# A mixture-of-experts layer in split precision: 14 expert blocks with 64 token rows, high and low parts side by side

## The chip, the cores and the metric

The kernel runs on one NeuronCore of a Trainium2 chip. Time is device microseconds from start to end of one execution; lower is better. One execution is recorded by the hardware profiler, instruction by instruction: PE is the matrix engine (TensorE), PEld its weight loads, DVE the vector engine, ACT the scalar engine, POOL the GpSimd engine, SP the engine that issues most DMAs.

## What is computed

One layer of a decoder on 512 tokens of 1024 features, all in float32: three kinds of attention, an output projection with residual, and then a mixture of experts with top 4 of 32 experts, residual and a final RMSNorm. The change touches the mixture alone:

```python
logits = (xf @ w_router + b_router)
top_v, top_e = lax.top_k(logits, 4); gates = jax.nn.softmax(top_v, axis=-1)
# for every expert e, over the tokens that chose it:
gu = xe @ w_gu[e] + b_gu[e]                  # 1024 -> 2048
gate = jnp.minimum(gu[..., 0::2], 7.0)
up = jnp.clip(gu[..., 1::2], -7.0, 7.0)
act = (up + 1.0) * (gate * jax.nn.sigmoid(gate * 1.702))
y = act @ w_dn[e] + b_dn[e]                  # 1024 -> 1024, times the gate, added to the token
```

The 2048 pairs of token and expert are spread unevenly: 38 to 177 tokens to an expert, 64 on average.

## The kernel before

**Precision.** A float32 product is made of three products in the format fp32r. Both factors are split: the high part is the value rounded to fp32r by a copy, the low part is what is left. `three` (lines 1319 to 1323) adds high x high, high x low and low x high into one PSUM bank of 512 columns. The token rows are the stationary factor, 128 rows wide; the weights stream through.

**Blocks.** An expert's tokens are cut into blocks of at most 128. Which block belongs to which expert is worked out on the core: DVE counts tokens (line 1122 on), numbers the blocks, and the tables `exp_i`, `tok_i`, `gate_t` and `y_row_i` tell for each block its expert, its tokens, their gates and where the rows of the result go. There are at least 32 blocks; `loops` is the number of the last one.

**Halves.** A block's weights come as 12 pieces of 128 x 2048, called halves: 8 of gate/up (one k tile of 128 rows each) and 4 of down (two k tiles each). Each goes the same way. SP loads it into one of six slots of `raw` (1 MB); ACT rounds it into one of four slots of `w_hi` (`hi_m`, line 605); DVE writes raw minus high into `w_lo` (`lo_m`, line 873); PE runs 12 matmuls with it (`gate_up` line 1576, `down` line 1619). `lo_ready` frees the raw slot and releases PE; `half_used` frees the w_hi and w_lo slot.

**One iteration b** of the loop over blocks runs, on every engine in an order written out by hand, the gate/up of block b and the down of block b - 1:

- PE (`one_block`, line 1644): 8 halves of gate/up into the four banks of `gu_psum`, after the third the eight transposes of `act` (`turn_acts`); the bias (`gu_bias`, then `gu_done`); the eight transposes of the next block's token rows (`turn_rows`); 4 halves of down into two banks of `turn_psum`. Before the next iteration it waits on `sig_ready`, for gate/up overwrites the banks that the sigmoid reads.
- ACT (lines 804 to 816): `hi_m` 4 to 6, the high part of the turned act (`turn_act`, two pieces), `hi_m` 7 to 11, the sigmoid, the high part of the turned tokens (`turn_x`), `hi_m` 12 to 15 (the first four of the next iteration), and `y_out`, which scales the down result by the gate into `y_row`.
- DVE (lines 1255 to 1268): `lo_m` 4 to 6, the low part of the turned act, `lo_m` 7 to 10, `clamp` (two passes over gate/up), `lo_m` 11, the low part of the turned tokens, `activate`, `lo_m` 12 to 15.
- POOL (lines 582 to 586): gathers the token rows of block b + 1, loads the biases of block b, and scatters `y_row` of block b - 1 to `expert_rows` when `y_free` says it is ready.

The last block and the sum of the four rows of each token follow the loop.

## Time and profile before

| | |
|---|---|
| runs | 1488.14 us median of 3 (1487.26 to 1488.17) |
| the profiled execution, first to last instruction | 1485.0 us, 21394 instructions |
| PE busy | 1443.0 us (97%), 7006 matmuls |
| DVE busy | 1304.8 us (88%) |
| ACT busy | 1017.6 us (69%) |
| POOL busy | 274.3 us (18%) |
| moved by DMA | 472.64 MB |

Busy time is the union of an engine's instructions; a matmul's own duration is longer than the distance to the next one, since they are pipelined. "Idle before, releaser" names what ended the wait. Granted clock 1.00 is TensorE's 2.4 GHz, 0.50 is 1.2 GHz. A DMA share is the busy share of the core's 16 DMA engines in a stretch; a packet counts where it ends, so it can pass 1.

### The profile page before, as it was taken

The page shows a single profiled execution, that of the slowest core. Times are in us where ns is not written, and L with a number is a line of the kernel's source. Part 1 is how long each engine was busy: PE and PEld are TensorE (multiplying, and loading weights), DVE is VectorE, ACT ScalarE, POOL GpSimd, SP SyncE. Part 2 cuts the span into 40 slices and gives each one's busy share as a digit, 9 for nine tenths or more (in the row PEclk, how much of TensorE's full clock was granted, in tenths as well). Part 3 has the DMA queues.
Part 4 walks back from the last instruction along what each step waited for, and adds up shares of the span by engine and source line. Part 5 has one row for each costly group of instructions (what it writes and reads, how often), then busy time and mean ns, then how long its engine had stood idle before and what let it go on. Part 6 is the DMA issues. An engine that isn't in the chain of part 4 may idle for free.

```text
span 1485.0 us, 21394 instructions
## 1 busy us (share of the span) xinstructions
PE 1443.0 (97%) x7006; PEld 1173.1 (79%) x7006; DVE 1304.8 (88%) x1230; ACT 1017.6 (69%) x913; POOL 274.3 (18%) x282
## 2 busy tenths in 40 slices
PE   6999999899999999999999999999999999999996
PEld 6877866878888888888888888888888888888883
DVE  7358575899999999999999999999999999999998
ACT  6344345377777777777777777777777777777772
POOL 0000000033222222222222232222222222222210
PEclk9999999899999999999999999999999999999998
DMA  9411130499999999999999999999999999999994
GB/s 349 143 58 57 34 142 15 180 327 391 377 388 375 373 379 374 376 367 372 367 370 375 375 377 365 377 377 378 376 377 377 375 375 375 370 377 362 373 378 178
DMA packets 102334, 472.64 MB, mean 318 GB/s; under 512 B 16499, under 2 KB 16539, under 8 KB 68000
## 3 DMA queue, kind: packets, MB, share of 16 engines
q1 hardware_dynamic: 87632, 451.71, 78.0%
q0 software_dynamic: 14672, 20.53, 3.9%
q8 instruction: 18, 0.29, 0.1%
q14 instruction: 12, 0.10, 0.0%
HBM read 467.70 MB, written 22.02 MB: 330 GB/s over the span
## 4 chain that ended last, share of the span: by engine, by line
PE 92%; DVE 6%; DMA 1%; ACT 1%; issue 1%; SPq 0%; DVEq 0%
PE gu_bank L1321 18%; PE gu_bank L1322 18%; PE gu_bank L1323 18%; PE turn_bank L1321 8%; PE turn_bank L1323 8%; PE turn_bank L1322 8%; PE bank L1608 2%; PE bank L1615 2%; PE bank L1321 1%; PE bank L1323 1%; PE bank L1322 1%; PE gu_bank L1461 1%; PE gu_bank L1601 1%; DMA arena<-in_x_dram 1%; DVE w_lo L873 1%; PE turn_bank L1487 1%
## 5 line engine op out<-in xcount | busy, mean ns | idle before, releaser
L873 DVE TENSOR_TENSOR w_lo<-raw,w_hi 128x2048 fp32r<-128x2048 f32 x411 | 931.7, 2289 | 98.3 <-ACT w_hi L605 93.5
L605 ACT ACTIVATE w_hi<-raw 128x2048 fp32r<-128x2048 f32 x411 | 784.6, 1920 | 209.1 <-PE gu_bank L1323 176.0
L1321 PE MATMUL gu_bank<-w_hi,turned 128*128 128x512 f32 x1080 | 423.8, 392 | 1.2 <-ACT arena L795 1.1
L1323 PE MATMUL gu_bank<-w_hi,turned 128*128 128x512 f32 x1080 | 420.5, 389 | 0.0
L1322 PE MATMUL gu_bank<-w_lo,turned 128*128 128x512 f32 x1080 | 420.4, 389 | 0.0
L1321 PEld LDWEIGHTS gu_bank<-w_hi,turned 128*128 128x128 f32 x1080 | 202.8, 188 | 43.6 <-ACT arena L795 1.4
L1323 PEld LDWEIGHTS gu_bank<-w_hi,turned 128*128 128x128 f32 x1080 | 202.7, 188 | 42.3
L1322 PEld LDWEIGHTS gu_bank<-w_lo,turned 128*128 128x128 f32 x1080 | 202.9, 188 | 40.7
L1321 PE MATMUL turn_bank<-w_hi,turned 128*128 128x512 f32 (+1 forms) x544 | 213.4, 392 | 0.0
L1323 PE MATMUL turn_bank<-w_hi,turned 128*128 128x512 f32 (+1 forms) x544 | 210.4, 387 | 0.0
L1322 PE MATMUL turn_bank<-w_lo,turned 128*128 128x512 f32 (+1 forms) x544 | 210.3, 387 | 0.0
L571 POOL DMA_INDIRECT expert_rows<-arena x32 | 58.9, 1841 | 811.0 <-ACT arena L778 785.6
L1323 PEld LDWEIGHTS turn_bank<-w_hi,turned 128*128 128x128 f32 x544 | 102.2, 188 | 20.8
L1321 PEld LDWEIGHTS turn_bank<-w_hi,turned 128*128 128x128 f32 x544 | 102.4, 188 | 19.9 <-issue 0.2
L1322 PEld LDWEIGHTS turn_bank<-w_lo,turned 128*128 128x128 f32 x544 | 102.3, 188 | 19.6
L546 POOL DMA_INDIRECT arena<-normed_rows,arena x32 | 77.8, 2432 | 29.1 <-POOL arena L543 25.9
L771 ACT ACTIVATE arena<-gu_bank 128x1024 f32<-128x1024 f32 x32 | 33.0, 1030 | 65.4 <-DVE arena L1213 65.4
L578 POOL DMA_DIRECT2D turned<-split_biases x128 | 66.8, 549 | 1.8 <-issue 1.8
L543 POOL COPY arena<-arena 128x1 int32 (+1 forms) x32 | 47.2, 1475 | 8.6 <-DVE arena L1168 7.3
L720 ACT ACTIVATE raw<-turn_bank 128x512 f32<-128x512 f32 (+5 forms) x32 | 17.3, 542 | 42.5 <-PE turn_bank L1487 42.4
L736 ACT ACTIVATE arena<-arena,stat 128x128 f32<-128x128 f32 (+3 forms) x48 | 26.6, 555 | 27.4 <-DVE stat L950 27.4
L760 ACT ACTIVATE turned<-bank 128x512 fp32r<-128x512 f32 x66 | 35.7, 598 | 10.0 <-PE bank L1553 8.4
(297 smaller groups left out, 1352.3 us busy)
## 6 DMA issues: line engine op xcount, KB each, us to landing
raw<-in_w_gate_up_dram SPq DMA_DIRECT2D x264, 1024.0 KB, 8.1
raw<-in_w_down_dram SPq DMA_DIRECT2D x132, 1024.0 KB, 8.9
raw<-in_w_in_dram SPq DMA_DIRECT2D x10, 1024.0 KB, 6.8
raw<-in_w_out_dram SPq DMA_DIRECT2D x4, 1024.0 KB, 5.0
raw<-expert_rows SPq DMA_DIRECT2D x4, 1024.0 KB, 6.4
raw<-in_w_mem_kv_dram SPq DMA_DIRECT2D x2, 1024.0 KB, 12.1
arena<-in_x_dram SPq DMA_DIRECT2D x1, 2048.0 KB, 13.7
arena<-in_position_tables_dram SPq DMA_DIRECT2D x1, 2048.0 KB, 18.0
```

The costliest lines, as they stand in the source:

```text
L543: pool.tensor_copy(idx_gather, tok_i[:, column]).then_inc(idx_ready, 1)
L546: pool.indirect_dma_start(h_row, None, h_dram, bass.IndirectOffsetOnAxis(idx_gather, 0), bounds_check=S - 1, oob_is_err=False).then_inc(h_ ...
L571: pool.indirect_dma_start(y_dram, bass.IndirectOffsetOnAxis(idx_scatter, 0), y_row, None, bounds_check=TOPK * S - 1, oob_is_err=False).the ...
L578: pool.dma_start(bias_now[c * E:c * E + 2, :].unsqueeze(1), bias_rows[:, bass.ds(e, 1), c // 2, c % 2, :]).then_inc(bias_now_in, 16)
L605: a.activation(home, raw_ap, ACT.Copy).then_inc(hi_ready, 1)
L760: a.activation(into[:, 4 * q:4 * q + 4, :], psum[6 + q][:, :].rearrange("p (k s) -> p k s", k=4), ACT.Copy).then_inc(xhi_ready, 1)
L771: a.activation(sig_t, gu_psum[:, :].rearrange("p (i two) -> p two i", two=2)[:, 0, :], ACT.Sigmoid, scale=ALPHA).then_inc(sig_ready, 1)
L873: v.tensor_tensor(home[1], raw_ap, home[0].bitcast(F32), ALU.subtract).then_inc(lo_ready, 1)
L1321: pe.matmul(bank, a[0], b[0], start=first, stop=False)
L1322: pe.matmul(bank, a[0], b[1], start=False, stop=False)
L1323: return pe.matmul(bank, a[1], b[0], start=False, stop=last)
L1608: ins = pe.transpose(psum[6 + k // 4][:, k % 4 * P:(k % 4 + 1) * P], h_row[:, k * P:(k + 1) * P], ident)
```

## The change

14 experts with at most 64 tokens (number 0 left out; if there are fewer such experts, others give their first 64 tokens) are made into narrow blocks of 64 rows. They take the odd places 1, 3, ... 27 in the order of blocks; wide ones take the even places and everything from 28 on. In a narrow block the 64 rows' high parts fill stationary columns 0 to 63 and their low parts columns 64 to 127 of the same tile. Two products, with the weights' high and low part (`two`), then give high rows in PSUM partitions 0 to 63 and low rows in 64 to 127. The low half is copied to SBUF by ACT and added onto the upper half by PE, with the matrix `half_back`, a one at (64 + j, j): four matmuls after gate/up (`fold_gate_up`), two after down (`fold_down`). The product low x low is added too.

The loop body becomes two iterations, one odd (`narrow_after_wide`: narrow gate/up, wide down) and one even (`wide_after_narrow`), with some others written out around it. In the odd one `clamp` on DVE stands behind `lo_m` 11 and `turn_x`, and the sigmoid behind `hi_m` 12. `y_out` of a narrow block is done early in the following odd iteration. POOL scatters two blocks back instead of one. The counting of blocks on DVE gets longer, and the constants grow from 525 to 687 columns.

The core of the diff:

```diff
+NARROW = 14
+NARROW_ROWS = P // 2
+LOOP_FROM = 2 * NARROW + 2
 # POOL
-            with pool.Fori(1, loops) as b:
+            pool.wait_ge(xtp_done, 2)
+            gather(slice(2, 3), 3)
+            bias_of_block(1)
+            with pool.Fori(2, loops) as b:
                 pool.wait_ge(xtp_done, b + 1)
-                gather(bass.ds(b + 1, 1), b * 2 + 1)
+                gather(bass.ds(b + 1, 1), b * 2)
                 bias_of_block(b)
-                scatter(b - 1, b * 2 + 2)
+                scatter(b - 2, b * 2 + 1)
 # ACT
+            def turn_x_narrow(q, n):
+                a.wait_ge(xtp_done, n)
+                a.activation(hx[:, 4 * q:4 * q + 4, 0:NARROW_ROWS], turned_rows[:, 4 * q:4 * q + 4, 0:NARROW_ROWS],
+                             ACT.Copy).then_inc(xhi_ready, 1)
+            def low_of_gate_up(n):
+                a.wait_ge(gu_done, n)
+                a.activation(gu_low, gu_psum[:, :], ACT.Copy).then_inc(gu_low_in, 1)
+            def low_of_down(used):
+                a.wait_ge(half_used, used)
+                a.activation(y_low, turn_psum[:, :], ACT.Copy).then_inc(y_low_in, 1)
+            def wide_after_narrow(b, narrow_next):
+                for i in range(4, 7):
+                    hi_m(GU + i, b)
+                turn_act_narrow(0, b)
+                turn_act_narrow(1, b)
+                for i in range(7, 12):
+                    hi_m(GU + i, b)
+                sigmoid(b + 1)
...
+                for i in range(12, 16):
+                    hi_m(GU + i, b)
+                low_of_down(b * 12 + (16 + GU))
+            def narrow_after_wide(b, folded):
+                hi_m(GU + 4, b)
+                if folded is not None:
+                    y_out_folded(folded, column(b - 2), b * 16)
+                hi_m(GU + 5, b)
+                hi_m(GU + 6, b)
+                turn_act(0, b)
+                turn_act(1, b)
+                for i in range(7, 11):
+                    hi_m(GU + i, b)
+                low_of_gate_up(b + 1)
+                hi_m(GU + 11, b)
+                turn_x(0, b + 2)
+                turn_x(1, b + 2)
+                hi_m(GU + 12, b)
+                sigmoid(b + 1, NARROW_ROWS)
+                for i in range(13, 16):
+                    hi_m(GU + i, b)
+                y_out(b * 12 + (16 + GU), column(b - 1), b * 16 + 16)
 # DVE
-            link(v.tensor_scalar(n_blk, count, float(P), 1.0, ALU.is_gt, ALU.add))
+            link(v.scalar_tensor_tensor(out=few, in0=count, scalar=NARROW_ROWS + 0.5, in1=cst[:, C_NOT_FIRST:C_NOT_FIRST + E],
+                                        op0=ALU.is_lt, op1=ALU.mult))
+            link(v.tensor_tensor_scan(few_seen, ones[:, 0:E], few, 0.0, ALU.mult, ALU.add))
...
+            def turn_x_narrow(q, n):
+                v.wait_ge(xhi_ready, n)
+                high = hx[:, 4 * q:4 * q + 4, 0:NARROW_ROWS]
+                v.tensor_tensor(hx[:, 4 * q:4 * q + 4, NARROW_ROWS:P], turned_rows[:, 4 * q:4 * q + 4, 0:NARROW_ROWS],
+                                high.bitcast(F32), ALU.subtract).then_inc(xlo_ready, 1)
+            def narrow_after_wide(b, folded):
...
+                for i in range(7, 12):
+                    lo_m(GU + i, b)
+                turn_x(0, b * 2 + 3)
+                turn_x(1, b * 2 + 4)
+                clamp(b + 1, folded)
+                lo_m(GU + 12, b)
+                activate(b + 1, b, NARROW_ROWS)
+                for i in range(13, 16):
+                    lo_m(GU + i, b)
 # PE
+            def two(bank, a, b, first=False, last=False):
+                pe.matmul(bank, a, b[0], start=first, stop=False)
+                return pe.matmul(bank, a, b[1], start=False, stop=last)
+            def fold_gate_up(n):
+                pe.wait_ge(gu_low_in, n)
+                for c in range(4):
+                    ins = pe.matmul(psum[c], half_back, gu_low[:, c * 512:(c + 1) * 512], start=False, stop=True,
+                                    skip_group_check=True)
+                ins.then_inc(gu_folded, 1)
+            def narrow_after_wide(b, n, between=None):
+                pe.wait_ge(xlo_ready, b * 2 + 2)
+                for k in range(GU):
+                    gate_up(k, GU + k, b, between=between if k == 0 else None, narrow=True)
+                    if k == 0 and between is None:
+                        fold_down(n - 1)
+                    if k == 2:
+                        turn_acts(b)
+                gu_bias(b, narrow=True)
+                pe.wait_ge(alo_ready, b * 2)
+                turn_rows(b * 16 + 16)
+                pe.wait_ge(y_free, b)
+                for j in range(DN):
+                    down(j, 2 * GU + j, b)
+                    if j == 0:
+                        fold_gate_up(n)
+            pe.wait_ge(sig_half, 1)
+            narrow_after_wide(1, 1, lambda: pe.wait_ge(sig_ready, 1))
+            with pe.Fori(1, NARROW) as n:
+                wide_after_narrow(n * 2)
+                b = n * 2 + 1
+                pe.wait_ge(sig_ready, b)
+                narrow_after_wide(b, n + 1)
+            wide_after_narrow(LOOP_FROM - 2)
+            wide_after_wide(LOOP_FROM - 1, NARROW)
+            with pe.Fori(LOOP_FROM, loops) as b:
+                wide_after_wide(b)
```

## Rows read from the trace of the kernel before

**Rows 1.** The page: busy us, share of the span, instructions.

```profile
span 1485.0 us, 21394 instructions
PE 1443.0 (97%) x7006; PEld 1173.1 (79%) x7006; DVE 1304.8 (88%) x1230; ACT 1017.6 (69%) x913; POOL 274.3 (18%) x282
```

**Rows 2.** Busy time by stretches: one block; columns in the first row.

```profile
core 0: us, PE busy (x) PEld busy (x) DVE busy (x) ACT busy (x) POOL busy (x), PEclk, DMA share, GB/s
1000.00:1035.00 35.00, 35.00 (x165) 28.79 (x164) 32.93 (x20) 26.79 (x20) 7.76 (x9) 1.00 0.96 376
```

**Rows 3.** DMA issues, the page: count, KB each, median us to landing.

```profile
raw<-in_w_gate_up_dram SPq DMA_DIRECT2D x264, 1024.0 KB, 8.1
```

**Rows 4.** Who waited for whom, 400 to 1400 us: us, times, longest.

```profile
ACT w_hi L605 <- PE gu_bank L1323: 153.3, 203, 0.8
```

**Rows 5.** Timeline of DVE, one block: start, us, instruction, idle before.

```profile
1012.28 1.22 DVE L1211 TENSOR_SCALAR arena<-gu_bank 128x1024 f32<-128x1024 f32 x1
1013.53 1.23 DVE L1213 SCALAR_TENSOR_TENSOR arena<-gu_bank,arena 128x1024 f32<-128x1024 f32 x1
1014.67 2.28 DVE L873 TENSOR_TENSOR w_lo<-raw,w_hi 128x2048 fp32r<-128x2048 f32 x1
1016.87 1.28 DVE L1194 TENSOR_TENSOR turned<-bank,turned 128x512 fp32r<-128x512 f32 x2
1018.07 1.22 DVE L1221 SCALAR_TENSOR_TENSOR arena<-arena 128x1024 f32<-128x1024 f32 x1
1019.20 11.20 DVE L873 TENSOR_TENSOR w_lo<-raw,w_hi 128x2048 fp32r<-128x2048 f32 x5
...
1047.30 1.22 DVE L1211 TENSOR_SCALAR arena<-gu_bank 128x1024 f32<-128x1024 f32 x1
```

**Rows 6.** Timeline of PE, two matmuls of a run with 32 between them.

```profile
699.64 0.39 PE L1321 MATMUL turn_bank<-w_hi,turned 128*128 128x512 f32 x1
...
707.12 0.39 PE L1321 MATMUL turn_bank<-w_hi,turned 128*128 128x512 f32 x1
```

**Rows 7.** Busy time by stretches: without and with POOL's transfers.

```profile
1003.50:1007.00 3.50, 3.50 (x17) 2.89 (x16) 3.00 (x2) 2.70 (x2) 0.00 (x0) 1.00 1.05 418
1028.00:1031.50 3.50, 3.50 (x19) 2.90 (x18) 3.29 (x3) 2.13 (x3) 2.44 (x2) 1.00 0.97 328
```

**Rows 8.** Groups of instructions of ACT, 320 to 1440 us: busy, mean ns.

```profile
L605 ACT ACTIVATE w_hi<-raw 128x2048 fp32r<-128x2048 f32 x384 | 733.5, 1920 | 196.2 <-PE gu_bank L1323 168.6 <-PE turn_bank L1323 24.8
L760 ACT ACTIVATE turned<-bank 128x512 fp32r<-128x512 f32 x62 | 33.5, 598 | 0.0
L771 ACT ACTIVATE arena<-gu_bank 128x1024 f32<-128x1024 f32 x32 | 33.0, 1030 | 65.4 <-DVE arena L1213 65.4
```

**Rows 9.** Timeline of ACT, the last halves before the sigmoid.

```profile
1010.84 1.92 ACT L605 ACTIVATE w_hi<-raw 128x2048 fp32r<-128x2048 f32 x1 [0.80 <-PE gu_bank L1323]
1014.79 1.03 ACT L771 ACTIVATE arena<-gu_bank 128x1024 f32<-128x1024 f32 x1 [2.04 <-DVE arena L1213]
```

**Rows 10.** The chain that ended last, 284 to 300 us: start, us, what.

```profile
286.81 0.23 DVE arena L1131
287.05 0.20 DVE arena L1133
...
288.93 0.18 DVE arena L1138
289.13 0.18 DVE arena L1139
...
293.00 0.61 DVE turned L1194
293.61 0.04 issue
293.65 0.50 PE gu_bank L1321
```

**Rows 11.** Busy time by stretches before the experts, for TensorE's clock.

```profile
184.00:188.00 4.00, 2.68 (x15) 2.18 (x15) 1.85 (x5) 0.00 (x0) 0.00 (x0) 1.00 0.00 0
196.00:200.00 4.00, 3.25 (x14) 1.95 (x14) 3.39 (x10) 1.20 (x6) 0.00 (x0) 0.80 0.92 373
276.00:280.00 4.00, 2.89 (x18) 2.75 (x17) 3.37 (x21) 1.77 (x1) 0.55 (x1) 0.61 0.35 132
280.00:284.00 4.00, 2.35 (x10) 2.21 (x10) 3.86 (x9) 2.48 (x9) 0.00 (x0) 0.50 0.13 52
```

More of the change, by code:

```diff
@@ L1581, in gate_up @@
                         between()
-                    ins = three(psum[c], (rows[0][:, k, :], rows[1][:, k, :]), w_part(slot, c * 512, (c + 1) * 512),
-                                first=k == 0)
+                    w = w_part(slot, c * 512, (c + 1) * 512)
+                    if narrow:
+                        ins = two(psum[c], hx[:, k, :], w, first=k == 0)
+                    else:
+                        ins = three(psum[c], (rows[0][:, k, :], rows[1][:, k, :]), w, first=k == 0)
                 ins.then_inc(half_used, 1)
@@ L1600, in gu_bias, with fold_down @@
                     rows = slice(c * E, c * E + 2)
[L1601 removed]
+                    ins = pe.matmul(psum[c], (ones_narrow if narrow else ones_r)[rows, :], bias_now[rows, :], start=False,
+                                    stop=True)
                 ins.then_inc(gu_done, 1)
+            def fold_gate_up(n):
[4 more added lines that the diff above has]
+                ins.then_inc(gu_folded, 1)
+            def fold_down(n):
+                pe.wait_ge(y_low_in, n)
+                for c in range(2):
+                    ins = pe.matmul(psum[4 + c], half_back, y_low[:, c * 512:(c + 1) * 512], start=False, stop=True,
+                                    skip_group_check=True)
+                ins.then_inc(y_folded, 1)
             def turn_rows(n_h):
@@ L1625, in down @@
                         at0 = kk * D + c * 512
-                        ins = three(psum[bank + c], (rows[0][:, k, :], rows[1][:, k, :]),
-                                    w_part(slot, at0, at0 + 512), first=k == 0, last=k == KT - 1)
+                        if narrow:
+                            ins = two(psum[bank + c], ha[:, k, :], w_part(slot, at0, at0 + 512), first=k == 0, last=k == KT - 1)
+                        else:
+                            ins = three(psum[bank + c], (rows[0][:, k, :], rows[1][:, k, :]),
+                                        w_part(slot, at0, at0 + 512), first=k == 0, last=k == KT - 1)
                 ins.then_inc(half_used, 1)
```

222 lines of the change are left out of this document (177 added, 45 removed).

## Prediction

> **What bounds the kernel now.** I read the page first, then the stage of the experts, then one block of it. The page gives a span of 1485.0 us with PE busy 97% and DVE 88% [rows 1]. The expert stage is 33 blocks (264 gate/up loads, eight per block [rows 3]) and is nearly all of the span from 294 us on. The view by stretches has PE busy for 35.00 of 35.00 us at full clock, DVE for 32.93 and ACT for 26.79; the DMA engines show a share of 0.96 [rows 2]. Who waits says the same: in 1000 us ACT waits 203 times on PE's matmuls in gu_bank, 153.3 us in all, because hi_m needs one of the four slots of w_hi back [rows 4]. So PE sets the pace, but DVE has only 2 us to spare in a block. The block repeats exactly: clamp starts at 1012.28 and at 1047.30, so a block is 35.02 us [rows 5]. On PE 33 matmuls lie between 699.64 and 707.12, a pitch of 0.2267 us, in all forms of the helper three [rows 6]; 144 of them are 32.6 us, and the two turns of eight transposes and the bias are the other 2.4.
>
> A second limit is closer than the shares look. In a stretch without POOL's transfers the DMA engines give 418 GB/s at share 1.05; in one with the gather and the scatter 328 GB/s at 0.97, and over the block 376 [rows 7]. I divide the block into 7 us at about the slower rate (two such stretches, 2.4 MB) and the other 10.8 MB at 418: 7 + 25.7 = 32.7 us. That is DMA's least time for a block; I call it an estimate.
>
> **How many blocks change.** I worked the routing out from the reference's inputs: the 32 experts get 38 to 177 tokens, one (number 1) over 128, which gives 33 blocks of 128 as the loads confirm. 19 experts other than number 0 have at most 64, the first 14 of them become narrow. Wide blocks left: 19 (experts 0, 1 twice, and the other 16). 19 + 14 = 33 again, so no weight load is saved or added: HBM's bytes stay, loops stays 32. Narrow gate/up falls in iterations 1, 3, ... 27, narrow down in 2, 4, ... 28. I count in pairs (odd, even iteration), 14 of them, each 70.04 us now.
>
> **PE in a pair.** A narrow block has two matmuls where there were three: 48 fewer, 48 x 0.2267 = 10.9 us. The folds add six matmuls of 512 columns at the same pitch, 1.4 us. PE's work falls from 70.0 to 60.5 us. If that were the time, 14 x 9.5 = 133 us would go. It isn't, for DVE's work is nearly unchanged: the weights are split into w_hi and w_lo as before.
>
> **DVE in a pair.** Pitches from one block [rows 5]: w_lo 2.22 (five of them 11.2), a turn of two halves 1.20, clamp 2.39, activate 1.13; 12 x 2.22 + 2 x 1.20 + 2.39 + 1.13 = 32.6. Clamp and activate on 64 partitions have the same 1024 elements in each, so I take them at the same price. Narrow turns have 256 elements instead of 512. Bounds for the pair of them: 1.20 (no gain) and 0.60 (half); I take 0.70. Four halves narrow: 1.0 us less per pair. DVE: 65.1 - 1.0 = 64.1 us. ACT gets low_of_gate_up (2048 elements from PSUM; the sigmoid's 1024 take 1.03 us and the turn's 512 0.60 [rows 8], so about 1.9) and low_of_down (1.0), less 0.9 for its narrow turns: 2 x 26.8 + 2.9 - 0.9 = 55.6, no bound.
>
> **The pair as it will run.** Four slots let DVE and ACT be three halves ahead at most, and PE is slow in the 12 wide halves in a row and fast in the 12 narrow ones. So I walked through one pair, with these pitches and one rule from the trace: hi_m starts when PE leaves the slot (1010.84), its w_lo starts 1.95 us later [rows 8, 9], so the slot is ready 4.2 us after PE left it. Clock 0 is the end of the odd iteration's w_lo number 7, with PE right behind it.
> Odd: PE ends number 7 at 1.9, the bias at 2.4 (gu_done). ACT copies the low rows 2.4 to 4.4. PE turns rows to 3.4, does number 8 to 6.1 and fold_gate_up to 7.0: the wait on gu_low_in costs nothing, since the copy lies beside number 8. DVE does 8 to 11 and turn_x by 10.1, clamp by 12.5, and ACT's sigmoid is ready at 13.5; PE finishes the wide down at 15.1. So sig_ready is in time by 1.6 us, although clamp has moved behind one w_lo and turn_x.
> Even: DVE and PE go side by side, PE number 7 at 38.1, DVE 0.8 us idle in two waits for slots, clamp 39.5 to 41.9, number 11 at 44.1. PE ends the narrow down at 46.8. DVE has turn_x_narrow and activate before number 0 of the next odd iteration, ready at 48.15: PE waits 1.4 us. Then fold_down waits for y_low_in: low_of_down is queued on ACT behind hi_m 12 to 15, and 15 needs PE's last slot (46.8), so with ACT still working off its queue the copy ends at 52.45. PE has ended number 0 at 50.0 and waits 2.5 us, and number 1 of the gate/up is queued behind it. ACT's hi_m 5 needs that slot: DVE loses 0.5 us there. Number 7 ends at 65.4. So the pair is 65.4 us; PE has 4.9 us of idle time in it and DVE 1.3.
> y_out_folded (1.2 us) stands behind hi_m 4 and delays hi_m 5 a little; it is in the walk.
> DMA's least time for a pair is 2 x 32.7 = 65.4 us, the same number by another way. Two engines without slack can't cover each other's waits, so I add 0.8 us (a third of DVE's idle time in one block now, 2.4 us): **66.2 us**. Bounds: 64.1 (DVE with no idle time) and 69.0 (next section).
>
> **Off the pair.** (1) Routing. The chain from DVE to the first gate/up matmul at 293.65 runs through DVE's small steps without a gap [rows 10]. Before it the change adds 13 steps of 32 to 48 columns or fewer (0.205 us each by 288.93 to 289.13), one reduce with its read (0.2), one unlinked compare (0.2) and two of 128 columns (0.30): 3.7 us, at least 3.3 and at most 4.2. past_ready, now at about 287.0, comes 1.8 us later, when PE is still in the first half of its gather matmuls: nothing. (2) number_blocks and split_biases get four steps; they hide beside PE's table and gate/up of block 0, and the first turn_x, now narrow, gives the time back. If that cover is gone they cost 1 us. (3) The constants grow by 162 columns, 0.08 MB, ahead of x on SP's queue: 0.2 us. (4) POOL's scatter now stands two blocks back and the gather in front of it; among ACT's waits now there is none on the scatter. With its wait on y_free already met it is sent when the bias loads are, and y_row is needed again most of a block later: nothing. POOL's wait on xtp_done holds up only POOL's own gather, bias loads and scatter. Sum: +3.9, say +4.0 us.
>
> **Sum.** 14 x (70.04 - 66.2) = 53.8 us less, 4.0 more: -49.8. Against the profiled span 1485.0 this gives 1435.2; the median of the runs is 1488.14, 3.1 above the span, and with the same 3.1 us the time is **1438.3 us**.
>
> **Rivals.**
> A, the forecast: pair 65.4 to 67.2, 1427 to 1452 us. Chance 0.50.
> B, weight loads become the bound at less than the rate I took. 376 GB/s at share 0.96 [rows 7] may be all but full; dividing by the share alone, 35.02 x 0.96 = 33.6, a pair 67.2, and with a share that stays at 0.98, 68.6. For it: the share. Against it: 418 GB/s in the clean stretches. 1452 to 1478, chance 0.22. DVE and ACT would then wait on raw<-in_w_gate_up_dram.
> C, DVE with no idle time at all, pair 64.1 to 65.4: 1409 to 1427, chance 0.09. PE's whole saving, pair 60.5: 1359; only if DVE's pieces became shorter; chance 0.01.
> D, the handovers of the two folds cost more than I walked: a pair of 69 to 70.3 us, 1478 to 1496. For it: each fold adds two crossings between engines, and all later halves queue behind it. Against: in the walk only one of the two is exposed. Chance 0.08.
> E, slower: TensorE's clock. PE now never rests in the stage. In the stage before the experts it does, and the granted clock was 1.00 with 2.68 of 4 us busy, 0.80 with 3.25, and 0.61 and 0.50 with 2.89 and 2.35 [rows 11], that is partly or wholly at 1.2 GHz. The new narrow stretch leaves PE about 15 of 19 us busy, with gaps of 1.4 and 2.5 us. At 1.2 GHz a 512-column matmul can't take under 0.427 us, 0.20 more. DVE covers 66.2 - 60.5 = 5.7 us, 28 such matmuls of the 96 in the stretch; from 49 on the pair is over 70.3 us and the kernel slower than before. All 96: pair 79.7, 14 x 9.7 + 4 = 139 us, 1627 us; half of them, about 1490. Chance 0.08.
> On this the Trainium skill, page "TensorE: Matmul & The Clock Gate", section "A second HAM failure mode: psum-queue depth-cycling", has a rule against the change: matmul groups broken by frequent short idle times make the clock swing between its two levels. By that rule case E holds; the row with 2.68 of 4 us busy at 1.00 speaks for small gaps being harmless.
> F, it doesn't do what it says: other narrow experts than I counted, so that a block more is run. 35 us more, 1473. Chance 0.02.
>
> **How the numbers follow.** Faster: A, B, C, half of D's range and F, 0.50 + 0.22 + 0.10 + 0.04 + 0.02 = 0.88. Within 0.2% (3 us, what a measurement of this kernel can just tell): D's end, 0.03. Slower: the rest of D and E, 0.09. The range 1412 to 1476 holds A, most of C and of B, and F.
>
> **What would show it.** In the profile after: pairs of sigmoids 66 us apart instead of 70 in the first 28 iterations, and 35.0 after that; DVE at 97% busy or more there; PE at about 91%, waiting on w_lo and once per pair, 2 to 3 us, on y_low; the granted clock 1.00; 396 weight loads as before; the first gate/up matmul at about 297.6 instead of 293.65. Wrong: "ACT waits for raw loads" high (B), clock under 1.00 in the stretches behind even iterations (E), a wait of PE on gu_low or on ACT's sigmoid of over 1 us (D), or the pair of narrow turns on DVE not at 0.7.

## The result and the profile after

The changed kernel takes **1438.18 us** (median of 4 runs, 1438.15 to 1442.28), the kernel before 1488.08 beside it: a ratio of **0.9675** (95% interval 0.9661 to 0.9688), faster by 3.25%. The forecast was 1438.3. The agreement to 0.1 us is luck in part: a pair gained more than forecast, one pair fewer gained, and the two cancelled.

The page of the changed kernel, to be read beside [rows 1] and [rows 3] (span; busy us, share of the span, instructions; then a DMA issue with KB each and median us to landing):

```profile
span 1436.5 us, 20084 instructions
PE 1333.8 (93%) x6418; PEld 1058.0 (74%) x6418; DVE 1282.2 (89%) x1252; ACT 1029.2 (72%) x941; POOL 426.8 (30%) x282
...
raw<-in_w_gate_up_dram SPq DMA_DIRECT2D x264, 1024.0 KB, 11.2
```

There are 588 fewer matmuls, that is 14 x 48 less 14 x 6 for the folds, and 264 gate/up loads as before: 14 narrow blocks, and no block more or less. A load now takes 11.2 us from issue to landing instead of 8.1. Busy time of 800 us in the part with narrow blocks, and of the wide blocks after it (us, then PE, PEld, DVE, ACT, POOL busy with counts, granted clock, DMA share, GB/s), to be read beside [rows 2]:

```profile
400.00:1200.00 800.00, 752.80 (x3476) 599.55 (x3477) 776.17 (x461) 662.60 (x489) 340.24 (x193) 1.00 1.00 398
1279.15:1384.16 105.01, 105.01 (x489) 86.19 (x488) 98.84 (x58) 80.44 (x58) 16.43 (x23) 1.00 0.95 372
```

The pace has passed from PE (94% busy now) to DVE (97%) and the DMA engines (share 1.00 at 398 GB/s). In the wide blocks PE is at 100% and three blocks take 105.0 us, 35.0 each as before. DVE's timeline has the clamps of wide blocks 2 and 28 of the changed kernel at

```profile
388.05 1.22 DVE L1373 TENSOR_SCALAR arena<-gu_bank 128x1024 f32<-128x1024 f32 x1
...
1244.21 1.22 DVE L1373 TENSOR_SCALAR arena<-gu_bank 128x1024 f32<-128x1024 f32 x1
```

and the same two of the kernel before at

```profile
381.86 1.22 DVE L1211 TENSOR_SCALAR arena<-gu_bank 128x1024 f32<-128x1024 f32 x1
...
1292.47 1.22 DVE L1211 TENSOR_SCALAR arena<-gu_bank 128x1024 f32<-128x1024 f32 x1
```

13 pairs took 910.61 us and take 856.16: a pair fell from 70.05 to **65.86 us**, where 66.2 was forecast. So the span's difference, 48.5 us, has four parts: the first gate/up matmul is 5.5 us later (293.65 in [rows 10], 299.12 now), of which 1.4 us do not come from the change (below, "The start"); the first pair gains nothing (to clamp 2 it is 88.2 us before and 88.9 after); 13 pairs give 54.5 back; the rest changes by 0.2.

One pair on DVE, timeline of the changed kernel (start, us, instruction; in brackets idle time before it and its releaser), beside [rows 5]:

```profile
716.50 1.22 DVE L1373 TENSOR_SCALAR arena<-gu_bank 128x1024 f32<-128x1024 f32 x1
...
721.09 0.75 DVE L1351 TENSOR_TENSOR turned<-bank,turned 128x256 fp32r<-128x256 f32 x2
721.75 1.22 DVE L1383 SCALAR_TENSOR_TENSOR arena<-arena 128x1024 f32<-128x1024 f32 x1
722.89 15.50 DVE L991 TENSOR_TENSOR w_lo<-raw,w_hi 128x2048 fp32r<-128x2048 f32 x7
738.30 1.28 DVE L1345 TENSOR_TENSOR turned<-bank,turned 128x512 fp32r<-128x512 f32 x2
739.50 8.89 DVE L991 TENSOR_TENSOR w_lo<-raw,w_hi 128x2048 fp32r<-128x2048 f32 x4
749.63 2.29 DVE L991 TENSOR_TENSOR w_lo<-raw,w_hi 128x2048 fp32r<-128x2048 f32 x1 [1.24 <-ACT w_hi L639]
...
753.03 1.21 DVE L1373 TENSOR_SCALAR arena<-gu_bank 64x1024 f32<-64x1024 f32 x1
```

Seven and four low parts stand without a gap. The gap of 1.24 us is a wait for ACT, and ACT's own timeline says where that came from: it waited for loads of down weights. Ahead of the first row DVE waited three times more for ACT, 0.24, 0.42 and 0.42 us, while PE did the wide gate/up and ACT waited for its slots.

```profile
738.45 1.92 ACT L639 ACTIVATE w_hi<-raw 128x2048 fp32r<-128x2048 f32 x1 [0.27 <-DMA raw<-in_w_down_dram]
741.01 1.92 ACT L639 ACTIVATE w_hi<-raw 128x2048 fp32r<-128x2048 f32 x1 [0.64 <-DMA raw<-in_w_down_dram]
744.10 1.92 ACT L639 ACTIVATE w_hi<-raw 128x2048 fp32r<-128x2048 f32 x1 [1.17 <-DMA raw<-in_w_down_dram]
745.92 1.87 ACT L815 ACTIVATE turned<-gu_bank 128x2048 fp32r<-128x2048 f32 x1
```

PE's timeline shows the two waits that the walk had put behind the narrow down:

```profile
725.23 0.50 PE L1535 MATMUL gu_bank<-w_hi,turned 128*128 128x512 f32 x1 [1.47 <-DVE w_lo L991]
...
728.75 0.72 PE L1833 MATMUL turn_bank<-turned 128*128 128x512 f32 x2 [1.42 <-ACT turned L820]
```

At the start of the experts PE stood idle, and the matmuls that followed came at a pitch of 0.43 us:

```profile
299.12 0.54 PE L1529 MATMUL gu_bank<-w_hi,turned 128*128 128x512 f32 x1 [3.82 <-DVE turned L1340]
299.46 0.62 PE L1530 MATMUL gu_bank<-w_lo,turned 128*128 128x512 f32 x1
299.88 0.63 PE L1531 MATMUL gu_bank<-w_hi,turned 128*128 128x512 f32 x1
```

### The profile page after: what moved, and what is told of

Same layout as the page of the kernel before. It is cut to its first block, busy times and chain, and to the rows that moved or that the text cites. A ratio compares the mean times of both kernels' runs of the same rounds, so it can differ in the third digit from the quotient of the medians.

```text
span 1436.5 us, 20084 instructions
## 1 busy us (share of the span) xinstructions
PE 1333.8 (93%) x6418; PEld 1058.0 (74%) x6418; DVE 1282.2 (89%) x1252; ACT 1029.2 (72%) x941; POOL 426.8 (30%) x282
## 4 chain that ended last, share of the span: by engine, by line
PE 44%; DVE 24%; issue 14%; DMA 9%; ACT 8%; DVEq 0%; SPq 0%; ACTq 0%
DVE w_lo L991 13%; PE gu_bank L1529 9%; PE gu_bank L1531 9%; PE gu_bank L1530 9%; DMA raw<-in_w_down_dram 8%; ACT w_hi L639 6%; DVE arena L1373 2%; PE turn_bank L1529 2%; PE turn_bank L1531 2%; PE turn_bank L1530 2%; PE bank L1529 2%; DVE arena L1383 1%; ACT turned L815 1%; PE bank L1531 1%; PE bank L1530 1%
## 5 line engine op out<-in xcount | busy, mean ns | idle before, releaser
L991 DVE TENSOR_TENSOR w_lo<-raw,w_hi 128x2048 fp32r<-128x2048 f32 x411 | 921.5, 2284 | 69.6 <-ACT w_hi L639 68.6
L601 POOL DMA_INDIRECT expert_rows<-arena x32 | 222.4, 6949 | 331.4 <-ACT arena L840 172.3
L1529 PE MATMUL gu_bank<-w_hi,turned 128*128 128x512 f32 x632 | 251.9, 399 | 12.3 <-DVE w_lo L991 8.3
L1531 PE MATMUL gu_bank<-w_hi,turned 128*128 128x512 f32 x632 | 247.0, 391 | 0.0
L1535 PE MATMUL gu_bank<-w_hi,turned 128*128 128x512 f32 x448 | 179.9, 402 | 29.6 <-DVE w_lo L991 28.2
L1529 PEld LDWEIGHTS gu_bank<-w_hi,turned 128*128 128x128 f32 x632 | 119.0, 188 | 47.6 <-DVE w_lo L991 16.9
L1531 PEld LDWEIGHTS gu_bank<-w_hi,turned 128*128 128x128 f32 x632 | 119.0, 188 | 25.4
L1535 PEld LDWEIGHTS gu_bank<-w_hi,turned 128*128 128x128 f32 x448 | 84.1, 188 | 60.6 <-DVE w_lo L991 42.4
L1529 PE MATMUL turn_bank<-w_hi,turned 128*128 128x512 f32 (+1 forms) x320 | 125.0, 391 | 0.0
L1531 PE MATMUL turn_bank<-w_hi,turned 128*128 128x512 f32 (+1 forms) x320 | 123.1, 385 | 0.0
L1530 PE MATMUL turn_bank<-w_lo,turned 128*128 128x512 f32 (+1 forms) x320 | 123.0, 384 | 0.0
L833 ACT ACTIVATE arena<-gu_bank 128x1024 f32<-128x1024 f32 (+1 forms) x32 | 32.9, 1027 | 80.8 <-DVE arena L1375 70.7
L1535 PE MATMUL turn_bank<-w_hi,turned 128*128 128x512 f32 x224 | 88.6, 395 | 0.0
L1536 PE MATMUL turn_bank<-w_lo,turned 128*128 128x512 f32 x224 | 87.2, 389 | 0.0
L608 POOL DMA_DIRECT2D turned<-split_biases x128 | 68.0, 543 | 22.9 <-issue 21.3
L1531 PEld LDWEIGHTS turn_bank<-w_hi,turned 128*128 128x128 f32 x320 | 60.1, 188 | 12.0
## 6 DMA issues: line engine op xcount, KB each, us to landing
raw<-in_w_gate_up_dram SPq DMA_DIRECT2D x264, 1024.0 KB, 11.2
```

Of the source, the lines that this page charges most:

```text
L601: pool.indirect_dma_start(y_dram, bass.IndirectOffsetOnAxis(idx_scatter, 0), y_row, None, bounds_check=TOPK * S - 1, oob_is_err=False).the ...
L608: pool.dma_start(bias_now[c * E:c * E + 2, :].unsqueeze(1), bias_rows[:, bass.ds(e, 1), c // 2, c % 2, :]).then_inc(bias_now_in, 16)
L833: a.activation(sig_t[0:rows, :], gu_psum[0:rows, :].rearrange("p (i two) -> p two i", two=2)[:, 0, :], ACT.Sigmoid, scale=ALPHA).then_inc( ...
L991: v.tensor_tensor(home[1], raw_ap, home[0].bitcast(F32), ALU.subtract).then_inc(lo_ready, 1)
L1529: pe.matmul(bank, a[0], b[0], start=first, stop=False)
L1530: pe.matmul(bank, a[0], b[1], start=False, stop=False)
```

## The experiments

The theory: in the narrow pairs DVE's work sets the pace, and the weight loads, now at their own limit, put short waits between its pieces; PE and the folds are off the path. The rivals: the loads alone are the bound; the handovers of the folds are; DVE alone is. For the start: PE's longer wait and the clock after it cost the time, or PE is not what sets the start. Each expectation names its own theories. The kernel before had 1487.37 us beside e1 to e4, 1487.84 beside e5 to e8 and 1487.57 beside e9 to e12.

**e1, three quarters of each load.**

```diff
-                sp.dma_start(raw[:, i % 6, :].rearrange("p (e n) -> p e n", e=1),
-                             gu_dram[bass.ds(e, 1), :, k, :]
+                cols = slice(0, 2 * D if isinstance(e, int) else 3 * D // 2)
+                sp.dma_start(raw[:, i % 6, :].rearrange("p (e n) -> p e n", e=1)[:, :, cols],
+                             gu_dram[bass.ds(e, 1), :, k, cols]
```

(and the down weights in the same way)

> Leaves out: in the loop over blocks the last quarter of every weight load (1.0 MB becomes 0.75 MB; the last columns of the slot are stale). Only DMA gets less to do. Theory 1 (a pair of iterations is paced by the hand-over between DVE, ACT and PE, 65.4 us by the walk, and the 0.5 to 0.9 us above that are ACT's waits for weights): the pair goes from 65.9 (mean of pairs 2 to 14 in the changed kernel) to about 65.2, all in all 7 to 12 us less than 1438.2, so 1426 to 1432; ACT's wait on the down loads (24.6 us in all) goes to near 0. Rival 2 (the loads alone are the bound): the pair falls to what PE and the exposed waits need, 62 to 63.5, 1385 to 1410.

Measured 1426.66 us (1425.51 to 1428.34), ratio 0.9596 (0.958 to 0.9612). The pair is 64.95 us. Busy time of the same 800 us in e1 (columns as above):

```profile
400.00:1200.00 800.00, 758.39 (x3530) 608.92 (x3529) 786.28 (x468) 669.44 (x496) 358.42 (x194) 1.00 0.88 308
```

No wait of ACT on a load is left in that stretch, and theory 1 holds. So in the changed kernel the loads cost 0.9 us in a pair, 11.5 us of the time in all. With them out of the way DVE is 98.3% busy; the 1.1 us in a pair in which it is not are waits for ACT's high parts (12.9 us in 36 times in the stretch), the ones that stand in the wide gate/up.

**e2, the low part over half the columns.**

```diff
-                lo(half if b is None else (b - 1) * 12 + half, (w_hi[:, half % 4, :], w_lo[:, half % 4, :]),
-                   raw[:, i % 6, :])
+                cols = slice(0, HALF if b is None else HALF // 2)
+                lo(half if b is None else (b - 1) * 12 + half, (w_hi[:, half % 4, cols], w_lo[:, half % 4, cols]),
+                   raw[:, i % 6, cols])
```

> Leaves out: in the loop over blocks the low part of the second half of each weight piece (w_lo over 1024 of 2048 columns, the rest stale). DVE's piece falls from 2.22 to about 1.15 us, its work in a pair from 64 to 38 us. Theory 1 with DMA's least time right behind (65.4 us by the estimate in the prediction): the pair falls by at most 0.6 us, since the loads don't get faster, 1428 to 1438. Rival 2 (DVE alone is the bound, the loads have room): the pair falls to 61.5 to 63, 1385 to 1400.

Measured 1443.08 us (1442.31 to 1444.15), ratio 0.9701 (0.9685 to 0.9718); pair 66.37. With DVE busy for 482 of 800 us the kernel is 5 us **slower** than the changed one (its fastest run, 1442.31, is above the slowest of the changed kernel, 1442.28): a miss of every forecast. Two things show. The loads are at their limit, share 1.00 with ACT waiting for them (e2's busy time; then who waited, us in all, times, longest):

```profile
400.00:1200.00 800.00, 755.02 (x3442) 612.11 (x3441) 482.21 (x457) 657.72 (x484) 123.61 (x193) 0.97 1.00 396
```

```profile
PE turn_bank L1834 <- ACT turned L820: 38.7, 12, 4.4
ACT w_hi L639 <- DMA raw<-in_w_down_dram: 42.1, 53, 1.9
```

And with DVE ahead, PE comes to the fold of the down result earlier, waits about 3.2 us for ACT's copy of the low rows instead of 1.4, and after most of these waits runs at half clock (e2's PE timeline, and the busy time of the stretch behind it):

```profile
730.69 1.22 PE L1834 MATMUL turn_bank<-turned 128*128 128x512 f32 x2 [3.97 <-ACT turned L820]
731.71 0.63 PE L1536 MATMUL gu_bank<-w_hi,turned 128*128 128x512 f32 x1
732.13 0.63 PE L1537 MATMUL gu_bank<-w_lo,turned 128*128 128x512 f32 x1
```

```profile
732.00:736.00 4.00, 4.00 (x11) 3.03 (x11) 1.23 (x1) 2.24 (x4) 1.06 (x1) 0.50 1.02 391
```

So "DVE alone" falls, for half of its work gone frees nothing. Of the 13 pairs the three without a matmul at half clock took 65.22, 65.46 and 65.64 us, the other ten 66.65 on average. That fits loads and clock together as the cause of the loss; e3 and e12 test the two on a kernel with shorter loads. e2 with the late fold of e12, which would show full loads with the clock at 1.00 throughout, was not run.

**e3, both edits (e1 and e2).**

> Leaves out what e1 and e2 leave out, together. Theory 1 (DVE and the loads are both the bound, one right behind the other): only now PE sets the pace, a pair of 60.5 us plus up to 1.4 us of exposed wait at fold_down, 14 x 4 to 5.4 us less than now: 1362 to 1384, far more than the sum of e1 and e2. Rival 2 (one of them alone was the bound): no more than the larger of e1 and e2. Rival 3 (the hand-overs at the folds set the pace): over 1410.

Measured 1414.57 us (1410.76 to 1416.1), ratio 0.9504 (0.9487 to 0.9521); pair 64.39, granted clock 0.98 over the stretch. It is faster than either edit alone, so neither limit is the whole bound, but the forecast of 1362 to 1384 is missed by 30 us and the time is that of rival 3 (the handovers at the folds, over 1410). The wait at the fold stands there again (26.3 us in 12 times), and a few matmuls behind one of 2.19 us the clock falls: in e3's PE timeline the pitch changes from 0.23 to 0.43 us.

```profile
654.02 0.73 PE L1835 MATMUL turn_bank<-turned 128*128 128x512 f32 x2 [2.19 <-ACT turned L821]
...
655.29 0.54 PE L1538 MATMUL gu_bank<-w_lo,turned 128*128 128x512 f32 x1
655.63 0.63 PE L1537 MATMUL gu_bank<-w_hi,turned 128*128 128x512 f32 x1
656.05 0.63 PE L1538 MATMUL gu_bank<-w_lo,turned 128*128 128x512 f32 x1
```

That happens in 11 of the 13 pairs. Behind the same wait of 2.19 us at 397.03 and at 718.69 us the clock stays. Busy time of 6 us behind the waits at 654.02 and at 718.69:

```profile
654.00:660.00 6.00, 5.97 (x20) 4.72 (x21) 2.03 (x3) 4.84 (x4) 1.06 (x1) 0.72 0.93 372
718.70:724.70 6.00, 6.00 (x30) 5.06 (x31) 2.73 (x3) 6.00 (x5) 1.06 (x1) 1.00 0.92 357
```

The two pairs at full clock take 63.02 us each, the other eleven 64.64 on average. So half clock behind the wait costs 1.6 us in a pair.

**e12, both edits and the fold of down one half later.** The fold stands behind half 1 instead of half 0, and ACT does `hi_m` 5 ahead of `y_out_folded`:

```diff
-                    if k == 0 and folded is not None:
+                    if k == 1 and folded is not None:
                         fold_down(folded)
...
                 hi_m(GU + 4, b)
+                hi_m(GU + 5, b)
                 if folded is not None:
                     y_out_folded(folded, column(b - 2), b * 16)
-                hi_m(GU + 5, b)
```

> Leaves out what e3 leaves out (a quarter of each load, half of each low part) and moves fold_down behind the second gate/up half as in e6. e3 missed its forecast: 64.4 us a pair instead of 60.5 to 62, with a wait of PE of 2.2 us on y_low in each pair and a granted clock of 0.974 instead of 0.989. Theory 1 (with DVE and loads out of the way the pair is PE's work, 60.5 us, plus the exposed wait of the fold, plus matmuls at 1.2 GHz behind that wait): with the wait gone the clock is back at 0.99 and the pair at 60.5 to 61.5, so 14 x 3 to 4 us less than e3: 1360 to 1375. Rival 2 (ACT with its two copies and 24 roundings, 56 us of work in a pair, holds PE up through the slots): the wait moves elsewhere, over 1400.

Measured 1374.14 us (1372.15 to 1375.64), ratio 0.9238 (0.9222 to 0.9253), pair 61.38. Busy time of e12:

```profile
400.00:1200.00 800.00, 795.48 (x3731) 646.92 (x3731) 523.32 (x495) 702.55 (x523) 132.97 (x208) 1.00 0.91 325
```

Against e3 only the places of the fold and of `y_out_folded` differ: its wait falls from 26.3 to 4.5 us, the clock is 1.00 again, and 40 us go. That shows what held e3 back, and the pairs of e3 divide it: of the 39.1 us in 13 pairs 11 x 1.62 = 17.8 are the half clock and 13 x 1.64 = 21.3 (63.02 less 61.38) the wait itself. Theory 1 holds: ACT, with its work in the pair unchanged, is no bound. It also measures PE's own work in a pair: 61.0 us (99.4% of 61.38), against 60.5 in the prediction.

**e6, the fold late, nothing left out** (the diff of e12 on the changed kernel).

> fold_down moves from behind the first to behind the second gate/up half of the narrow block, y_out_folded on ACT from behind hi_m 4 to behind hi_m 5. PE's exposed wait on y_low (18.7 us in 14 pairs) goes. Theory 1: PE had room there, so 0 to 7 us, 1431 to 1438. Rival (the wait is passed on to DVE in full): 14 x 1.4 = 19 us less, 1419.

Measured 1437.78 us (1434.61 to 1440.92), ratio 0.9663 (0.9643 to 0.9684), pair 65.87: no change, as theory 1 had it. PE waits for w_lo instead (33.0 us in 24 times where it was 24.2). The same edit is worth 40 us where PE is the bound and nothing where DVE and the loads are.

**e4, no folds.** It leaves out both folds, ACT's two copies of the low rows and the waits on them.

```diff
-                    if j == 0:
-                        fold_gate_up(n)
...
-                low_of_gate_up(b + 1)
...
-                low_of_down(b * 12 + (16 + GU))
```

> Leaves out both folds: the low halves are neither copied by ACT nor added by PE, so the results of narrow blocks lack their low rows. PE loses six matmuls and the wait of 1.4 us on y_low per pair, ACT two copies of 2.9 us. Theory 1: PE has 5 us to spare in a pair and DVE and the loads keep the pace: 0 to 0.5 us per pair, 1431 to 1438. Rival D of the prediction (the hand-overs of the folds cost the pair 2 us or more): under 1412.

Measured 1438.69 us (1437.11 to 1439.55), ratio 0.967 (0.9654 to 0.9686), pair 65.96. Six matmuls, 2.9 us of ACT and four crossings between engines cost nothing, and rival D (the handovers) falls. ACT's waits on loads grow from 19.7 to 49.4 us in the 800 us: what ACT saves it spends there.

**e5, a third product in the narrow blocks**, so that PE has as many products as before and the folds besides.

```diff
-                return pe.matmul(bank, a, b[1], start=False, stop=last)
+                pe.matmul(bank, a, b[1], start=False, stop=False)
+                return pe.matmul(bank, a, b[0], start=False, stop=last)
```

> Adds a third product to every narrow tile, a repeat of the first (so the results of narrow blocks are too large by one product); everything else of the change stays. Theory 1 (the whole gain is the third matmul that is left out, and the new structure by itself costs): PE's work in a pair is 60.5 + 10.9 = 71.4 us and PE sets the pace again: 14 x (71.4 - 65.9) = 77 us more than 1438.2, about 1515, with waits at the folds up to 1530, slower than the kernel before by 27 us or more. Rival 2 (part of the gain comes from the new order of ACT and DVE): under 1500.

Measured 1519.31 us (1517.38 to 1520.09), ratio 1.0206 (1.0189 to 1.0223), pair 71.92, PE busy for 797.58 of 800 us. The whole gain is the 48 matmuls in a pair that are not done; the rest of the change alone costs 31 us.

**e7, seven narrow blocks** (`NARROW = 7`).

> Seven narrow experts instead of 14 (19 experts have at most 64 tokens, so the count of blocks stays 33). Theory: a fixed loss ahead of the loop (7 us by the traces: first matmul of iteration 1 at 329.3 instead of 322.3) and a gain per pair of 70.04 - 65.9 = 4.1 us: 7 pairs fewer, 29 us more, 1467. If the gain were not per pair (a better start or end, say) the time would stay nearer 1438.

Measured 1467.92 us (1464.84 to 1468.13), ratio 0.9866 (0.9849 to 0.9882). The first seven pairs bring 19.9 us, the other seven 30.0. Seven times 4.19 (70.05 less 65.86) are 29.3, so the gain goes by pairs, and the first seven bear a fixed cost of about 9 us: 4.1 for the longer routing and 4.9 in the first pair, which gains nothing (below).

**e8, the first low part of the turned tokens ahead of the routing's last steps.** PE's first gate/up matmul waits for it.

```diff
+            v.wait_ge(xhi_ready, 1)
+            v.tensor_tensor(la[:, 0:4, :], psum[6][:, :].rearrange("p (k s) -> p k s", k=4),
+                            ha[:, 0:4, :].bitcast(F32), ALU.subtract).then_inc(xlo_ready, 1)
             link(v.tensor_tensor(picked_slot, picked, slots.unsqueeze(2).to_broadcast([P, NT, TOPK, E]), ALU.mult))
```

> DVE does the low part of block 0's first token rows right after the slots are computed, before the 512-element product and the three 768-element steps, instead of behind them. Theory 1 (TensorE waits 3.8 us for exactly this step, and its clock falls to half for the next nine matmuls of block 0): the first gate/up matmul comes at about 295.4 instead of 299.1, at full clock (pitch 0.23 instead of 0.43 us), 3 to 5.5 us less, 1432.7 to 1435. Rival 2 (DVE has so much to do for block 0 that the wait comes back at the table or at w_lo 2): 0 to 1 us less.

Measured 1437.73 us (1436.97 to 1438.86), ratio 0.9662 (0.9646 to 0.9678): no change. The first gate/up matmul comes at 295.49 instead of 299.12 and runs at full clock, yet clamp 2 is only 1.3 us earlier (386.77) and the last clamp is where it was (1384.27 against 1384.16). Even the 1.3 us are not the edit's: e6 and e7, whose start is that of the changed kernel, have clamp 2 at 386.20 and 386.87. So what is gained at PE's start is not kept.

**e10, the kernel before with 20 more small steps on DVE ahead of that place.**

```diff
+            for _ in range(20):
+                link(v.tensor_copy(slot_i, y_at))
```

> The kernel before with 20 more small steps on DVE (16 columns, 0.205 us each) ahead of the routing's slots: 4.1 us. Theory 1 (the fixed loss of the change is the longer routing, plus TensorE's clock at half for the first nine matmuls of block 0 because PE waits longer): 4.1 us by the steps and up to 1.8 us by the clock, 1492 to 1493.8, with a matmul pitch of 0.43 us at the first gate/up. Rival 2 (DVE catches up in block 0, the steps are hidden): within 1 us of 1488.

Measured 1492.76 us (1491.33 to 1493.52), ratio 1.0031 (1.0019 to 1.0043), 5.2 us more, as theory 1 had it. The routing steps of 0.2 us each do reach the end, and with them the same wait and the same half clock as in the changed kernel, here in the kernel before (PE's timeline):

```profile
298.91 0.57 PE L1323 MATMUL gu_bank<-w_hi,turned 128*128 128x512 f32 x1 [3.95 <-DVE turned L1196]
299.28 0.63 PE L1324 MATMUL gu_bank<-w_lo,turned 128*128 128x512 f32 x1
299.70 0.63 PE L1325 MATMUL gu_bank<-w_hi,turned 128*128 128x512 f32 x1
```

From the first gate/up matmul to clamp 1 it is 54.99 us in e10 and 53.35 in the kernel before, with DVE busy for 51.88 and 51.89 us of them: where PE sets the pace, the half clock costs 1.6 us in the profiled execution. The medians leave 1.0 us for it (5.2 less 4.2 for the steps).

**e11, the edit of e8 on the kernel before.**

> The kernel before with e8's edit alone: the low part of block 0's first token rows ahead of the 512- and 768-element steps. In the changed kernel this gave nothing that can be told (1437.7 against 1438.2). Theory 1 (there the loads and DVE set the pace behind it, so an earlier start of PE is lost again; here PE sets the pace and keeps it): 2 to 4 us less, 1484 to 1486. Rival 2 (DVE's total work in block 0 sets the start of block 1 in both): 0 to 1 us less.

Measured 1490.63 us (1487.95 to 1491.63, 10 runs), ratio 1.0021 (1.0011 to 1.003): 3 us slower, against both theories. The trace is that of the fastest of the ten runs, 1487.95, whose span is only 1.3 us longer than the 1485.0 of the kernel before; it can explain that much and not the 3 us. The first gate/up matmul is 0.7 us earlier (292.98), but DVE now waits for ACT's high part in the middle of its steps (e11's DVE timeline).

```profile
289.84 0.69 DVE L1136 TENSOR_TENSOR turned<-bank,turned 128x512 fp32r<-128x512 f32 x1 [2.89 <-ACT turned L760]
```

Busy time from 288 to 292 us, in e11 and then in the kernel before:

```profile
288.00:292.00 4.00, 4.00 (x35) 3.83 (x35) 2.09 (x4) 0.60 (x1) 0.00 (x0) 1.00 0.98 387
```

```profile
288.00:292.00 4.00, 4.00 (x35) 3.82 (x34) 3.69 (x10) 0.60 (x1) 0.00 (x0) 1.00 1.00 387
```

DVE loses 1.6 us of work there and clamp 1 is 1.4 us later (348.41 against 347.0). So a first matmul that comes earlier is worth nothing if DVE's work behind it comes later. From 292 us on DVE is busy for 51.54 of 53 us in the kernel before, and PE for 51.82: neither has room, and e10 shows that PE's clock counts there too.

**e9, the changed kernel with the late fold and the edit of e8.**

> The changed kernel with e6's and e8's edits together, nothing left out, all results complete. If both were hidden behind the loads as their runs say, 1436 to 1438, no different from the changed kernel; if they add up, down to 1434.

Measured 1437.53 us (1435.86 to 1441.9), ratio 0.9666 (0.9645 to 0.9687): not to be told from the changed kernel. No kernel here that does the whole computation beats it.

## Why the prediction was right

**The bound and the pair: right, and for the stated reason.** Case A holds. PE's whole saving (named in case C) did not come, because DVE and the loads took over. e5 shows that the saving is PE's, e1 that the loads hold the pair by 0.9 us, e2 that DVE alone does not hold it, and e3 with e12 that with both relieved it falls to PE's work. The terms:

| term, us in a pair | forecast | measured |
|---|---|---|
| PE's work | 60.5 | 61.0 (e12) |
| DVE's work | 64.1 | 63.9 (776.17 of 800, times 65.86) |
| ACT's work | 55.6 | 54.5 |
| narrow turns on DVE, two | 0.70 | 0.66 (721.09 to 721.75) |
| copy of the low gate/up rows | 1.9 | 1.87 |
| walk without waits on loads | 65.4 | 64.95 (e1) |
| waits on loads, two engines without slack | 0.8 | 0.9 (65.86 less 64.95) |
| pair | 66.2 | 65.86 |

The walk was 0.4 us long. The 0.8 us had been the weakest term, a third of an idle time of another kind; e1 agrees with its size, but a third of 2.4 us had no row behind it, and that it came out is luck. The clamp on 64 partitions took 1.21 us where on 128 it takes 1.22: equal price, as assumed.

**The order of the walk: right in each place, one size off.** PE waited 1.47 us for w_lo in front of the odd iteration (1.4 forecast) and then at the down fold for 1.42 us (2.5 forecast). The term that was mis-sized is the queue of high parts in front of `low_of_down`: I took 1.95 us each, while ACT did four in a row in 7.33 us, 1.83 each. Four of them are 0.5 of the 1.1 us; the rest I have not followed. In e3 the clock falls behind a wait of 2.19 us in 11 of 13 pairs, so a gap of the size that I had forecast lies where case E begins. I gave E 0.08 and named the right place, but had no row that told a gap of 1.4 from one of 2.5. As for what E would have cost, the half clock was worth 1.6 us in a pair in e3, not the 10 to 19 us of 48 to 96 slow matmuls: behind one wait five to twelve were slow. (With 4.0 us of fixed cost the kernel would also have been slower from a pair of 69.8 us on, not 70.3.)

**The clock: right.** It was granted at 1.00 over the 800 us with all the gaps of up to 1.5 us in them. On this the Trainium skill ("TensorE: Matmul & The Clock Gate", section "A second HAM failure mode: psum-queue depth-cycling") has frequent short idle times between groups of matmuls as a cause of a clock that swings. The 1.00 of this kernel speaks against it for gaps of 1.4 to 1.5 us, two to a pair. In e2 and e3, with one gap of 2.2 to 4.4 us in each pair, the clock does swing (0.97 and 0.98 on average).

**Rival B, the loads: the estimate was near, but low.** I had 65.4 us as least time for a pair's loads and allowed up to 68.6. At share 1.00 the changed kernel runs a pair in 65.86 and e2 in 66.37; with full loads no kernel had a mean under 65.86. Single pairs did (the three of e2, 65.22 to 65.64), but in the changed kernel too they spread from 65.18 to 66.31. Dividing by the share alone (67.2) was too much, for the share did go to 1.00 and the rate from 376 to 398 GB/s. The least time of the loads by themselves was not measured.

**PE's share.** It was forecast at 91% and is 94% in the stretch of 800 us. PE's work was half a us more than counted, and busy time includes the tail of the last matmul ahead of each gap (a matmul's record lasts 0.39 us at a pitch of 0.23).

**The start: the routing right, the first pair overlooked.** I had 4.0 us of fixed cost. The routing chain itself came as counted: from 284.85 (line 1229) to 298.46 it is 13.6 us; before it was 9.6, from 283.44 (line 1111) to the same turn of the tokens at 293.00 [rows 10]. That is 4.05 more where 3.7 was forecast.

The chain also began 1.4 us later, but that is not the change. Up to that line e10 and e11 are the kernel before, and in them it begins at 284.50 and 283.16; in the other traces with the changed kernel's start it begins between 283.19 and 285.12. I can't say what sets it: from 284 to 288 us the granted clock is 0.50 in the changed kernel (284.85) and in e7 (283.80) alike.

PE's wait grew to 3.82 us, and nine matmuls at 0.43 us (1.2 GHz, granted clock 0.64 in 300 to 304 us) followed, which was not in the sum. In the changed kernel they cost nothing that can be seen at clamp 2. e7 has the same start with a wait of 2.98 us and keeps full clock, and from its first gate/up matmul to clamp 2 it takes 88.83 us, against 88.93.

What the sum lacked is that the first pair gains nothing, where I counted 14 pairs alike: 88.9 us to clamp 2 against 88.2. DVE's work ahead of clamp 2 is not less than before, and from 292 us on it was busy for 51.54 of 53 us already; but so was PE (51.82). That DVE is the reason is argued from this and from e8 and e11, not shown by a run of its own, and how the loss divides between DVE's added steps and the loads stays open.

**Why the number agrees.** 53.8 less 4.0 was forecast, 49.8. Measured are 54.45 in 13 pairs, less 0.7 for the first pair, less 4.05 for the routing, and 0.2 gained at the end: 49.9, which is what the medians differ by. The fixed cost was right; 13 pairs of 4.19 us less 0.7 happen to be the 14 of 3.84 that I had counted, and that is luck. The spans differ by 48.5 only, for the 1485.0 of [rows 1] is the span of a fast execution: it lies 3.1 us under the median time, while in every run whose time and span are both known the two differ by 1.6 to 1.8 us (1438.17 and 1436.5 for the changed kernel). The 1.4 us between these is as much as its chain began early. By adding the 3.1 us I started from the median in effect, so that the forecast does not suffer from it.

## What to carry to other kernels

When an engine that sets the pace loses work, walk one period with the pitches of the next engine and of the loads, and count instances one by one: the first pair gained nothing here. Loads that need almost as long as the engines do cost a little even so (0.9 us in a pair of 66 here). Compare the starts of two traces only after looking at how much the same code varies between executions (283.2 to 284.5 us for one line here), and compare medians with medians. A wait at the head of PE's queue costs nothing while PE is not the bound, but where PE is the bound it costs twice if the clock falls behind it (1.64 us for the wait and 1.62 for the clock, in a pair of e3); so place a fold behind work that is ready, above all in a kernel in which PE is the bound (40 us between e3 and e12).

## What the runs showed of the hardware

**Less work, more time.** Half of DVE's low parts left out made the kernel 5 us slower (e2), with a longer wait of PE and a clock of 0.97 instead of 1.00.

**The clock and single gaps.** PE waits of 1.42 and 1.47 us left it at 1.00. At or soon after waits of 2.19 us (11 of 13 in e3), 3.82 (the start), 3.95 (e10) and 3.97 us (e2) five to twelve matmuls of 512 columns came at a pitch of 0.43 instead of 0.23 us. But the length of the wait alone does not decide it: two waits of 2.19 us in e3 and three in e2 left the clock at 1.00, and so did 2.98 us (e7) and 3.04 us (e6) at the start, while 2.54 us there (e3) did not. e6's first gate/up matmul, and the busy time behind it:

```profile
298.21 0.50 PE L1529 MATMUL gu_bank<-w_hi,turned 128*128 128x512 f32 x1 [3.04 <-DVE turned L1340]
298.20:302.20 4.00, 3.99 (x18) 3.31 (x19) 3.79 (x11) 0.88 (x1) 0.00 (x0) 1.00 0.23 71
```

**POOL's scatter lasts until DVE's low parts let it through.** The group of `scatter`'s indirect DMA between 400 and 1200 us (count, then busy us and mean ns, then idle time before), in the kernel before, the changed kernel and e2:

```profile
L571 POOL DMA_INDIRECT expert_rows<-arena x22 | 40.9, 1859 | 557.5 <-ACT arena L778 532.1 <-issue 25.4
L601 POOL DMA_INDIRECT expert_rows<-arena x25 | 195.4, 7814 | 247.4 <-ACT arena L826 136.2 <-ACT arena L840 100.0 <-issue 11.2
L601 POOL DMA_INDIRECT expert_rows<-arena x25 | 26.5, 1061 | 293.6 <-ACT arena L840 146.5 <-ACT arena L826 137.9 <-issue 9.2
```

In e2 the loads are at share 1.00 too, so it is not the DMA engines: what differs is DVE, busy half as long. In e1, with DVE as busy and loads at 0.88, the mean is 7233 ns. In the pair above the scatter starts at 732.69 and takes 6.63 us, to 739.32, and DVE's run of seven low parts ends at 738.39; the next one ends at 772.97, and DVE's run at 772.04. All 25 scatters of the changed kernel in the stretch end 0.93 to 0.94 us after the last low part of such a run. What follows the low parts there, without a gap, is a turn, which reads PSUM and one tile in SBUF, so a busy DVE is not enough to hold the scatter up.

In the kernel before all 22 scatters end 0.93 to 0.94 us after a low part too, but after the first one that ends, in the middle of a run. There the low parts stand 0.01 to 0.04 us apart, while in the changed kernel each starts 0.08 us before the end of the last, as the sums of two show (DVE's timelines, before and changed; one takes 2.29 us):

```profile
1025.81 4.60 DVE L873 TENSOR_TENSOR w_lo<-raw,w_hi 128x2048 fp32r<-128x2048 f32 x2
731.70 4.49 DVE L991 TENSOR_TENSOR w_lo<-raw,w_hi 128x2048 fp32r<-128x2048 f32 x2
```

The Trainium skill says why this can be ("GPSIMD Engine Reference", section "1. Specifications"): GpSimd shares its SBUF interfaces with VectorE, and they contend when a VectorE instruction has two inputs in SBUF, as the low part has (raw and w_hi). The rows agree, with the turn as the instruction that has one input there. In e1 two of 25 scatters got through between two low parts without a gap (2.38 and 2.37 us), which stays open. No other engine waits for the scatter here; in a kernel where somebody does, it is an instruction that can last as long as DVE's unbroken row of such instructions beside it.
